# Three-part float32 products in twelve layers on one core: the first two chunks of each MLP taken together, and the order of ScalarE's roundings at the stage ends

## What is computed

```python
def sq_relu_mlp(u, w_up, w_down):                 # w_up 1024 x 4096, w_down 4096 x 1024
    return jnp.square(jax.nn.relu(u @ w_up)) @ w_down

# first block: four layers
h = h + rmsnorm(mixer(rmsnorm(h, gain_0)), gain_1)
h = h + rmsnorm(sq_relu_mlp(rmsnorm(h, gain_2), w_up, w_down), gain_3)
# second block: two layers, the outputs of mixer and MLP are added as they are
x = x + mixer(rms_norm(x, gain))
x = x + squared_relu_mlp(x, gain, w_up, w_down)
```

## Time and profile before

| | |
|---|---|
| median of 3 runs | 2296.12 us (2295.16 to 2296.16) |
| profiled execution, whole | 2296.52 us |
| its span, first to last instruction | 2294.7 us |
| TensorE busy | 2221.9 us, 97% of the span, 11634 matmuls |
| VectorE busy | 1492.1 us, 65% |
| ScalarE busy | 1197.5 us, 52% |
| GpSimd busy | 223.7 us, 10% |
| mean granted clock of TensorE | 0.982 of full speed |
| share of the 16 DMA engines taken by the weight queue | 47.9% |

### The profile page before, as it was taken

One profiled execution on the slowest core, in us unless ns is written; L12 is line 12 of the kernel. 1 busy time (PEld: TensorE's weight loads), 2 busy tenths in 40 slices (PEclk: granted clock), 3 DMA queues, 4 the chain that ended last, 5 costly groups with the idle time before them and its releaser, 6 DMA issues.

```text
span 2294.7 us, 29472 instructions
## 1 busy us (share of the span) xinstructions
PE 2221.9 (97%) x11634; PEld 1879.1 (82%) x11634; DVE 1492.1 (65%) x2081; ACT 1197.5 (52%) x1819; POOL 223.7 (10%) x204
## 2 busy tenths in 40 slices
PE   7999999999999999999999999978999999999999
PEld 7878888977888878889878888757888888798887
DVE  6645655887666767667636666785655898454665
ACT  5555544746445645455555444654444666455443
POOL 0001000652000020000001000001000000162000
PEclk9999999999999999999999999978999999899999
DMA  7535566514555436555545655523665666302553
GB/s 252 184 129 156 194 197 192 165 37 126 192 191 183 150 110 204 184 190 187 165 147 154 201 189 184 171 68 106 197 195 177 187 179 190 111 1 92 185 192 119
DMA packets 201528, 368.93 MB, mean 161 GB/s; under 512 B 6943, under 2 KB 142495, under 8 KB 201392
## 3 DMA queue, kind: packets, MB, share of 16 engines
q1 hardware_dynamic: 197776, 358.70, 47.9%
q0 software_dynamic: 3616, 8.35, 2.1%
HBM read 365.97 MB, written 1.05 MB: 160 GB/s over the span
## 4 chain that ended last, share of the span: by engine, by line
PE 87%; DVE 6%; ACT 4%; issue 1%; POOL 1%; DMA 0%; SPq 0%; DVEq 0%; ACTq 0%
PE PS L656 46%; PE PS L783 14%; PE PS L780 6%; PE PS L767 6%; PE PS L936 2%; PE PS L1257 2%; ACT whi L1313 2%; DVE wlo L1861 1%; PE PS L800 1%; PE PS L1226 1%; PE PS L857 1%; PE PS L801 1%; PE PS L1028 1%; PE PS L782 1%; POOL wlo L2714 1%
## 5 line engine op out<-in xcount | busy, mean ns | idle before, releaser
L1861 DVE TENSOR_TENSOR wlo<-raw,whi 128x1024 fp32r<-128x1024 f32 x658 | 791.8, 1229 | 200.3 <-ACT whi L1313 199.3
L1313 ACT ACTIVATE whi<-raw 128x1024 fp32r<-128x1024 f32 x680 | 699.7, 1055 | 379.7 <-PE PS L656 319.9
L783 PE MATMUL PS<-U,whi 128*128 128x512 f32 x1440 | 508.6, 397 | 5.0 <-DVE wlo L1861 5.0
L656 PE MATMUL PS<-whi,U 128*128 128x512 f32 x1728 | 483.4, 396 | 9.6 <-DVE U L2313 3.4
L656 PEld LDWEIGHTS PS<-whi,U 128*128 128x128 f32 x1728 | 322.5, 189 | 83.7 <-issue 14.3
L780 PE MATMUL PS<-U,wlo 128*128 128x256 f32 x1260 | 353.5, 281 | 0.0
L783 PEld LDWEIGHTS PS<-U,whi 128*128 128x128 f32 x1440 | 264.7, 188 | 58.4 <-issue 6.7
L656 PE MATMUL PS<-wlo,U 128*128 128x512 f32 x864 | 267.8, 391 | 0.0
L1988 DVE TENSOR_TENSOR AR<-PS,AR 128x512 f32<-128x512 f32 x96 | 66.3, 691 | 306.4 <-ACT AR L1400 306.3
L656 PE MATMUL PS<-whi,fH 128*128 128x512 f32 x832 | 258.1, 391 | 0.9 <-DVE fL L2124 0.9
L656 PE MATMUL PS<-whi,fL 128*128 128x512 f32 x832 | 256.3, 389 | 0.0
(11 more groups left out here) (322 smaller groups left out, 2454.3 us busy)
## 6 DMA issues: line engine op xcount, KB each, us to landing
raw<-in_mlp_w_up SPq DMA_DIRECT2D x64, 1024.0 KB, 5.5
raw<-in_mlp_w_down SPq DMA_DIRECT2D x64, 1024.0 KB, 5.0
raw<-in_ret_w_in SPq DMA_DIRECT2D x48, 1024.0 KB, 5.2
raw<-in_m_w_up SPq DMA_DIRECT2D x32, 1024.0 KB, 5.5
raw<-in_m_w_down SPq DMA_DIRECT2D x32, 1024.0 KB, 4.9
raw<-in_kv_w SPq DMA_DIRECT2D x24, 1024.0 KB, 5.3
raw<-in_ret_w_out SPq DMA_DIRECT2D x16, 1024.0 KB, 4.9
raw<-in_gla_w_in SPq DMA_DIRECT2D x12, 1024.0 KB, 5.2
```

What stands on the lines that cost most here:

```text
L656: mm = e.matmul(bank(b + nb), a, w[:, nb * 512:(nb + 1) * 512], start=(begins and n < 2), stop=(ends and n >= 4))
L783: mm = e.matmul(o, w_h[:, k, :], U[:, k, :, :, :], start=(k == 0), stop=(k == 7))
L1313: e.activation(split_half(whi, i, x), a, ACT.Copy).then_inc(HI.tick((i, x)), 1)
L1861: e.tensor_tensor(split_half(wlo, i, x), a, split_half(whi, i, x).bitcast(F32), ALU.subtract).then_inc(LO.tick((i, x)), 1)
```

## The change

- `gemm_up_two` replaces `gemm_up_first` and the first `gemm_up` in the MLPs. It takes chunks 0 and 1 together: `upper` is `whi` times both parts of U for one half s and one group of rows tt (8 matmuls of 256 columns), `lower` is `wlo` times the rounded part, for both groups of rows at once (8 matmuls of 256 columns). The order is upper (chunk, half, rows) (0,0,0), (0,1,0), (1,0,0), turning the second rows, (1,1,0), (0,0,1), (0,1,1), lower of chunk 0, (1,0,1), (1,1,1), lower of chunk 1. `upper` waits for the rounded half alone.
- Product 1 moves to banks 2 and 3, where the old `y` of the second rows stands. So before `upper(1,0,0)` TensorE waits for the two reads of it (`YG`, `YSQ`), or for the finished `h` where nothing is normed. The first down product waits for the sum of product 1 (`MX[S, 1]`).
- ScalarE, at each seam: the rounding of chunk n + 1 goes ahead of the turned second rows; where `y` is normed its first half stands between the squares and the square root of the second rows (`between`).
- In the MLP, third chunk: ScalarE rounds it behind its copy of product 0, ahead of rounding the squared result, and VectorE takes its remainder behind the square of product 0, ahead of `fL`.

```diff
--- before.py
+++ after.py
@@ -209,7 +209,7 @@
 
         def up_bank(f):
 
-            return 4 + 2 * (f % 2) if f else 0
+            return 2 * f if f < 2 else 4 + 2 * (f % 2)
 
         def up_chunk(S, f):
             return first[S] + (2 * f - 2 if f >= 2 else f)
@@ -802,6 +802,50 @@
                         if tt == 1:
                             mm.then_inc(USED.tick((i, s)), 1)
 
+            def gemm_up_two(S):
+
+
+                i0 = first[S]
+
+                def upper(f, s, tt):
+                    e.wait_ge(*HI[i0 + f, s])
+                    w, b = split_half(whi, i0 + f, s), up_bank(f) + s
+                    o = PS[:, b * 512 + tt * 256:b * 512 + tt * 256 + 256]
+                    for k in range(8):
+                        if f == 0 and s == 0 and k % 2 == 0:
+                            e.wait_ge(*UL[(S, "in"), tt, k // 2])
+
+                        e.matmul(o, w[:, k, :], U[:, k, tt, :, :], start=(tt == 0 and k == 0), stop=False, skip_group_check=True)
+
+                def lower(f, s):
+                    e.wait_ge(*lo_cut(i0 + f, s))
+                    w, b = split_half(wlo, i0 + f, s), up_bank(f) + s
+                    o = bank(b).rearrange("p (t l n) -> p t l n", t=2, l=2)[:, :, 0, :]
+                    for k in range(8):
+                        mm = e.matmul(o, w[:, k, :], U[:, k, :, 0, :], start=False, stop=(k == 7), skip_group_check=True)
+                    mm.then_inc(USED.tick((i0 + f, s)), 1)
+
+
+                upper(0, 0, 0)
+                upper(0, 1, 0)
+
+                if S - 1 in NORMED:
+                    e.wait_ge(*YG[S - 1, 1, 0])
+                    e.wait_ge(*YSQ[S - 1, 1, 1])
+                else:
+                    e.wait_ge(*HN[S, 1, 1])
+                upper(1, 0, 0)
+                turn_in(S, 1)
+                upper(1, 1, 0)
+                upper(0, 0, 1)
+                upper(0, 1, 1)
+                lower(0, 0)
+                lower(0, 1)
+                upper(1, 0, 1)
+                upper(1, 1, 1)
+                lower(1, 0)
+                lower(1, 1)
+
             def rows_of_r(S, dg, b):
                 e.wait_ge(*DIAG[S])
                 if S == RET0:
@@ -818,14 +862,11 @@
                         return fH[:, f % 3, o:o + 128], fL[:, f % 3, o:o + 128]
                     return of
 
-                for f in range(16):
-                    if f == 0:
-                        gemm_up_first(up_chunk(S, f), up_bank(f), (S, "in"))
-                    else:
-                        gemm_up(up_chunk(S, f), up_bank(f), [MX[S, f - 2]] if f >= 2 else [])
-                    if f >= 2:
-                        gemm_a((S, "y"), down_chunk(S, f - 2), 2, ap(f - 2), (0, 2), fresh=lambda k, tt: [FL[S, f - 2]],
-                               begins=(f == 2), ends=False)
+                gemm_up_two(S)
+                for f in range(2, 16):
+                    gemm_up(up_chunk(S, f), up_bank(f), [MX[S, f - 2]])
+                    gemm_a((S, "y"), down_chunk(S, f - 2), 2, ap(f - 2), (0, 2), fresh=lambda k, tt: [FL[S, f - 2]],
+                           free=([MX[S, 1]], [MX[S, 1]]), begins=(f == 2), ends=False)
                 gemm_last(S, lambda k, tt: ap(14 + k // 2)(k % 2, tt), lambda k, tt: [FL[S, 14 + k // 2]])
 
             def pe_ret(S):
@@ -1301,16 +1342,20 @@
         def act_program(e):
             done = [0]
 
+            def hi_half():
+
+                i, x = divmod(done[0], 2)
+                done[0] += 1
+                if x == 0:
+                    e.wait_ge(*landed(i))
+                if i >= NS:
+                    e.wait_ge(*USED[i - NS, x])
+                e.activation(split_half(whi, i, x), raw_halves(i)[x], ACT.Copy).then_inc(HI.tick((i, x)), 1)
+
             def hi_to(n):
 
-                while done[0] < min(n, NCH):
-                    i = done[0]
-                    done[0] += 1
-                    e.wait_ge(*landed(i))
-                    for x, a in enumerate(raw_halves(i)):
-                        if i >= NS:
-                            e.wait_ge(*USED[i - NS, x])
-                        e.activation(split_half(whi, i, x), a, ACT.Copy).then_inc(HI.tick((i, x)), 1)
+                while done[0] < 2 * min(n, NCH):
+                    hi_half()
 
             def hi_of(i0, n):
 
@@ -1363,7 +1408,7 @@
                     e.activation(junk[:, :], h[:, tt, :], ACT.Square, accum_out=st[:, tt:tt + 1]).then_inc(SQ.tick((S, tt)), 1)
                 root((S, "r"), st[:, 2:4])
 
-            def y_squares(S, tt):
+            def y_squares(S, tt, between=lambda: None):
                 e.wait_ge(*(YSQ[S, 0, 1] if tt else SQ[S, 1]))
                 e.wait_ge(*rows_done((S, "y"), tt))
                 for j in range(2):
@@ -1372,12 +1417,14 @@
                     ss = st[:, 8 + 2 * tt + j:9 + 2 * tt + j]
                     e.activation(junk[:, 512 * j:512 * j + 512], bank(2 * tt + j), ACT.Square,
                                  accum_out=ss).then_inc(YSQ.tick((S, tt, j)), 1)
+                between()
                 tmp = st[:, 22 + tt:23 + tt]
                 e.wait_ge(*MS[S, "y", tt])
                 e.activation(tmp, tmp, ACT.Sqrt, scale=st[:, 26 + tt:27 + tt] if S in MLPS else 1.0 / 1024,
                              bias=st[:, 201:202]).then_inc(RT.tick((S, "y", tt)), 1)
 
             def seam(S):
+
 
                 n = first[S + 1]
                 if S in NORMED:
@@ -1385,9 +1432,9 @@
                 hi_to(n + 1)
                 next_in(S + 1, 0)
                 if S in NORMED:
-                    y_squares(S, 1)
+                    y_squares(S, 1, between=hi_half)
+                hi_to(n + 2)
                 next_in(S + 1, 1)
-                hi_to(n + 2)
                 squares(S + 1)
 
             def act_mlp(S):
@@ -1398,6 +1445,8 @@
                         e.wait_ge(*MX[S, f - 2])
                     a = bank(up_bank(f), 2).rearrange("p (s l n) -> p s l n", s=4, l=2)
                     e.activation(m_t[f % 2].rearrange("p (s n) -> p s n", s=4), a[:, :, 1, :], ACT.Copy).then_inc(MT.tick((S, f)), 1)
+                    if f == 0:
+                        hi_of(up_chunk(S, 1), 1)
                     if f >= 2:
                         hi_of(down_chunk(S, f - 2), 1)
                     if f >= 3:
@@ -1989,6 +2038,8 @@
                                     m_t[f % 2].rearrange("p (s n) -> p s n", s=4), ALU.add).then_inc(MX.tick((S, f)), 1)
                     e.wait_ge(*MX[S, f])
                     e.scalar_tensor_tensor(x, x, 0.0, x, ALU.max, ALU.mult).then_inc(MQ.tick((S, f)), 1)
+                    if f == 0:
+                        lo_of(up_chunk(S, 1), 1)
                     if f >= 2:
                         lo_of(down_chunk(S, f - 2), 1)
                     e.wait_ge(*FH[S, f])
```

## The result

| | before | after |
|---|---|---|
| median (4 runs each, taken together) | 2296.14 us (2295.16 to 2296.37) | 2275.76 us (2274.81 to 2276.63) |
| profiled execution, its span | 2296.5, 2294.7 | 2274.8, 2273.0 |
| PE busy | 2221.9 us | 2205.2 us |
| mean granted clock | 0.982 | 0.986 |

The ratio of the medians is 0.9912, with a 95% interval of 0.9895 to 0.9929: faster by 20.4 us, where the forecast was 14.8. The sign, the part that the MLPs have in it and most marks in the trace are as predicted. Most of what is missing in the sum lies outside the MLPs.

The account below looks back on a forecast made before the run. TensorE, holding 87% of the chain, bounds the kernel. Gains of 9.0 (MLP0 to MLP3), 5.1 (MLP4, MLP5) and 0.8 (DIFF) make 14.9 off 2296.5: 2281.6, median 0.4 below, 2281.3 us; range 2277 to 2287.5.

Parts of the forecast that it names:

- rival C: The MLP entry was not on the path, so the time would be 2296; chance 0.03.
- the columns: MLP entries: chunk 0's remainders in 16 matmuls instead of 32, 1.92 us per MLP less 0.08, about 10.8 in all.
- the third chunk: In the MLPs TensorE's wait for VectorE's remainders there goes (0.77 in MLP0; 5.0 us in all six before).
- the cover of 0.45: Third chunk in MLP0: first half of the remainders ready at 14.05 us, TensorE comes at 14.52, 0.45 to spare.
- The down chunk's cover: First down chunk in MLP0: remainders ready at 20.0 us, chunk begins at 20.20; spare 0.2, the thinnest.
- Rival A: Third or down chunk remainders come late, each MLP gives back up to 0.9, 5.4 together; 2287.5; chance 0.16.
- the entries: First matmul to first down chunk: 2.17 us saved in MLP0 to MLP3 (MLP1 0.35 more), 2.56 in MLP4 and MLP5.
- The new wait in MLP0: Ahead of the seventh matmul, TensorE waits 0.92 us for the last quarter of the first rows.
- The root: ScalarE's square root in MLP0's entry slips 0.49 us behind the inserted half, from 2.32 to 2.81.
- Rival B: ScalarE's new order delays h rows by 1.03 us instead of 0.49 in eight normed seams; 8.3 back, 2290; chance 0.07.
- Rival D: The clock falls to 1.2 GHz in the entries: 8.8 us more each, 53 over six, 2334; chance 0.03.
- DIFF: An earlier norm factor removes TensorE's 0.90 us wait for the third chunk's remainders there; 0.8 taken.

Follow-up runs that it names:

- e4: The changed kernel with chunk 0's remainders multiplying both parts of U again (512 columns instead of 256): 2288.29 us, ratio 0.9968 to the kernel before.
- e3: The changed kernel without the early rounding and remainder of each MLP's third chunk, done at the old place: 2286.74 us, ratio 0.9965 to the kernel before.
- e6: The changed kernel with both halves of chunk n+1's rounding behind the square root: 2280.89 us, ratio 0.9933 to the kernel before.
- e2: The kernel before with ScalarE's new order only ahead of CONV, GLA, RET1, DIFF and DIL: 2292.47 us, ratio 0.9986 to the kernel before.
- e1: The changed kernel with ScalarE's new order only at the six seams ahead of an MLP: 2278.94 us against 2295.57 for the kernel before, 0.9931.
- r_before_8: The kernel before with 8 idle matmuls (1.8 us) in RET1: 2296.15 us, ratio 1.0 to the kernel before.
- v5: The changed kernel with chunk 0's products by quarters of U and, in CONV, twelve TensorE taps ahead of its wait for GpSimd's chain: 2272.68 us.
- s_before_12: The kernel before with 12 idle matmuls (2.7 us) in RET0: 2298.39 us, ratio 1.0013 to the kernel before.

## Why the prediction was right and where it was wrong

**Right: the path.** The end moved with the entries, so rival C is out.

**Right: the columns.** 10.5 by e4, 10.8 said. Chunk 1's 48 products of 256 columns cost what its old form did.

**Right: the third chunk.** The waits are gone, the cover of 0.45 was about 0.5. The down chunk's cover was not 0.2 but about 0.6: its first products are with `whi`, and I asked for the remainder at its first matmul. Rival A had its chance from that cover, and e3 shows what it would have cost (more than its 5.4).

**Right, with small terms off: the entries.** MLP0 to MLP3 gave 2.36, 2.73, 2.29 and 2.38 where 2.17 and once 2.52 were said, MLP4 and MLP5 2.58 and 2.57 for 2.56. The new wait in MLP0 is listed as 0.61, not 0.92, and is the same step: the listed idle time counts from the modelled end of the six (1.03), mine from where a dense row would go on (0.72), and the seventh matmul starts at 1.64 from T by both. The root slipped by 0.32 (2.64 from 2.32), not 0.49, so the turn ended at 5.03 and not 5.31; the turned rows took 0.1 of that back, and the third chunk came 0.17 sooner. It took 5.61 and not 5.68. Together 0.24. Rival B is out: the root slipped by 0.32 and not by 1.03, the turn shows one gap of 0.3 (1.32 for 1.04), and with e6's order the entries are longer. Rival D is out as well: the window of MLP0's entry, T to the down chunk, which answers to the earlier trace rows, has the clock at 1.00 again.

```profile
222.30:242.26 19.96, 19.31 (x137) 17.51 (x136) 16.91 (x35) 14.42 (x30) 7.83 (x9) 1.00 0.63 192
```

**Right in kind, mis-sized: DIFF.** Its wait went from 0.90 to 0, by e2 too. I took 0.8 for it; to the mark the new order gives 1.33. Listed idle time leaves out the tail of the group before (1.06 from where the dense row would go on), and 0.3 come from products ahead of it, as in DIL.

**Wrong: "In CONV, GLA, RET1 and DIL no wait hangs on it and I take 0."** For GLA and RET1 it holds (0.04, 0.02). In CONV a wait does hang on it, through three engines: norm factor, VectorE's first values, GpSimd's taps, TensorE's wait of 5.26 at the chain's end, some 65 us behind its start. I looked for waits near the seam; the row with "issue" in the waits of PE was there to be followed. It is worth 0.83, by the chain's start and by the wait, which e1 brings back. In DIL 0.30 hangs on it. So the order was worth 2.45 outside the MLPs where I had 0.8. The bound of 1.1 held what the order gave in CONV and in DIL.

**Wrong: no term for the clock outside the entries.** The forecast read the clock in MLP0's entry and nowhere else. DIFF's window in before, and in after, show it:

```profile
1440.00:1586.00 146.00, 123.36 (x557) 97.41 (x557) 109.75 (x192) 80.81 (x156) 0.67 (x1) 0.84 0.35 115
```

```profile
1424.00:1571.00 147.00, 119.77 (x566) 94.81 (x566) 112.44 (x200) 81.72 (x161) 2.19 (x2) 0.88 0.35 115
```

At 0.84 about a third of the time ((1 - 0.84) / 0.5) passes at the lower of the two levels (1.2 GHz, half of the upper), and a part of that changes with the stage's start, as r_before_8 shows. With the code of after in these stages, they differ by up to 2.3 us in CONV (138.13 to 140.45), 1.2 in DIFF (150.35 to 151.59) and 1.6 in DIL (334.02 to 335.62). The change fell well in all three, and that is luck: of CONV's 1.43, 0.6 is place, of DIFF's 2.12, 0.8, and of DIL's 1.81, 1.5. These 2.9 us, which no step of mine held, and 1.37 at the start (below), beside 0.8 in the MLPs and 1.7 by the order, are the 6.8 us by which the profiled execution beat my 14.9. The low end of the range allowed 1.1 each in CONV, GLA, RET1 and DIL, for the order alone. CONV and DIL gave 1.43 and 1.81, and DIFF 2.12 where I had 0.8.

**The start.** RET0's 1.37 are the profiled execution's. The transfer of the input landed 1.0 sooner, the first products begin 0.86 sooner, and they come 0.12 apart behind 16 of them instead of 22. The profile lists a clock of 1.00 here; I take the lower level from the distance of 0.21, as in the earlier trace rows. PE in before, the end of the dense row that the earlier trace rows stands in, and in after:

```profile
17.58 0.33 PE L801 MATMUL PS<-U,wlo 128*128 128x256 f32 x1
```

```profile
12.07 0.58 PE L800 MATMUL PS<-U,whi 128*128 128x256 f32 x1 [4.89 <-DVE wlo L1910]
...
15.44 0.39 PE L801 MATMUL PS<-U,wlo 128*128 128x256 f32 x1
```

This code is the same in both, and in the twelve executions without idle matmuls in RET0 it lies between 220.1 and 222.1, whichever version they are. So what the change is shown to give by its own steps is 14.9 + 2.45, or 17.4 us.

**What stays open.** How much of the other 3.0 in the median (20.4 - 17.4) belongs to this kernel for good. By three starts each (medians less the idle work: 2296.1, 2295.7, 2294.4 for before and 2275.8, 2277.4, 2279.1 for after) the difference is 18.0 on the mean, between 15.2 and 20.4. That the clock falls where it does because of TensorE's pauses is shown for CONV alone, where v5 moved a pause; no run here took those of DIFF and DIL away. Why the place changes as it does stays open too: 2.7 us ahead of the old order (s_before_12) left CONV, DIFF and DIL within 0.2 of before, and 1.8 us (r_before_8) took 0.7 off DIFF and 1.2 off DIL.

The Trainium skill (TensorE: Matmul & The Clock Gate, Part 1, on oscillation) says that a kernel whose TensorE pauses again and again pays the lower clock again and again. This case's traces agree as to the lower clock, 0.84 in DIFF with its many waits and 1.00 in MLP0's entry; what it costs goes by whether TensorE is waited for, much in DIL (2.9 us for six matmuls beside 1.56) and nothing in DIFF's middle. What the page would have changed in my sum is the width of the range: it gives no size for a shift of such a stage, and the rows give 1 to 2 us for each.

## What to carry to other kernels

Leaving out products and filling a pause with the next chunk's products paid to within 6% of what counting matmuls and tracing semaphores by hand said (14.9 for 14.1); that method can be trusted for the stretch that is edited. Follow each edited order to the end of the longest chain that starts there, also on engines that the diff does not touch, and take every long wait whose releaser is "issue" as a chain to be followed. Look at the granted clock of every stage first: where one runs below full speed, add 1 to 2 us of range for it on either side, and do not credit an edit with what one comparison shows there. Where such a stage is to be compared all the same, compare it up to a product ahead of its slow stretches, or behind a wait that takes them up: there all profiles with the same order agreed within 0.2 us, where whole stages differed by up to 2.4.

## What the runs showed of the hardware

The same instructions of a stage that runs partly at the lower clock took 334.0 to 335.6 us (DIL) or 138.1 to 140.5 us (CONV, both with the order of after), with other work ahead of them; 1.8 us of idle matmuls ahead of them cost 0.2 us in one kernel, and 2.7 us cost 4.3 in another (2280.06 against 2275.76). A stretch at the lower clock costs half of its length where TensorE works through it (CONV: 1.2 us more of it, 0.6 us later) and nothing where TensorE waits for another engine behind it (DIFF's middle, 23.78 us at a granted clock of 0.52 or 0.77). Moving a pause of TensorE in CONV moved the stretch (v5). Weight loads in the MLP entries are listed with 188 to 192 ns each, while rows of 256-column matmuls, each with a load of its own, ran 0.12 us apart: as listed, the loads overlap each other and the products, and the 0.12 per product holds them.
